# An expert layer in units of 32 rows: GpSimd makes the table of own rows, and TensorE turns the activation before the next rows

## What is computed

```
def hier_moe(h, w_rg, w_re, w_gate, w_up, w_down):
    ...
    act = jax.nn.silu(jnp.einsum('nd,edf->nef', xf, w_gate)) * jnp.einsum('nd,edf->nef', xf, w_up)
    act = act * comb.astype(act.dtype)[..., None]
    return jnp.einsum('nef,efd->nd', act, w_down).reshape(b, t, dm)
```

## Time and profile before

| what | value |
| --- | --- |
| median of three runs | 1614.38 us |
| the profiled execution | 1609.06 us, span 1607.3 us |
| TensorE matmul busy, whole span | 1386.7 us (86%) |
| VectorE busy | 682.8 us (42%) |
| GpSimd busy | 247.9 us (15%) |
| mean granted TensorE clock | 0.931 |
| weights and other loads of SyncE's hardware queue | 329.63 MB, 53.9% of 16 engines |
| loop over units | from about 1045 to 1584 us |
| gate/up matmuls (L2509) | 3328, 220.2 us |
| adds to x (L2597) | 156, 1215 ns each |

### The profile page before, as it was taken

How to read it: one execution, slowest core, us unless ns; L and a number is a source line. 1 busy time by engine, 2 the same in 40 slices (tenths; PEclk the granted TensorE clock), 3 DMA queues, 4 the chain that set the end, 5 groups by cost and what they waited for, 6 DMA issues and landing times. The chain is left out here.

```text
span 1607.3 us, 27516 instructions
## 1 busy us (share of the span) xinstructions
PE 1386.7 (86%) x10524; PEld 857.5 (53%) x10524; DVE 682.8 (42%) x1199; ACT 330.3 (21%) x734; POOL 247.9 (15%) x176
## 2 busy tenths in 40 slices
PE   7999999998999798778999899587889878887554
PEld 4478887777888566544544664433334333333221
DVE  3154333433553455574100223525455545654225
ACT  3001001222433244474000222111011111111102
POOL 0000000003000000000000000055344534453230
PEclk9999999999998699798999999789899989998877
DMA  9244547434430477104932234788958899859995
GB/s 346 104 171 168 188 146 259 149 120 171 172 112 7 144 233 233 47 1 172 310 111 105 96 114 187 298 321 367 377 245 326 353 421 375 367 191 418 421 422 217
DMA packets 108676, 360.96 MB, mean 225 GB/s; under 512 B 16462, under 2 KB 44150, under 8 KB 80290
## 3 DMA queue, kind: packets, MB, share of 16 engines
q1 hardware_dynamic: 104866, 329.63, 53.9%
q0 software_dynamic: 3232, 22.16, 3.8%
q10 hardware_dynamic: 512, 8.26, 1.4%
HBM read 482.68 MB, written 17.05 MB: 311 GB/s over the span
## 5 line engine op out<-in xcount | busy, mean ns | idle before, releaser
L2509 PE MATMUL bank<-ring,hT_e 128*32 128x256 f32 x3328 | 220.2, 415 | 87.6 <-DMA ring<-in_w_exp_up 50.1
L2597 DVE TENSOR_TENSOR x<-x,bank 128x1024 f32<-128x1024 f32 x156 | 183.1, 1215 | 262.8 <-PE bank L2496 256.7
L2465 POOL COPY ring<-ring 128x2048 f32 x104 | 194.9, 1902 | 246.8 <-DMA ring<-in_w_exp_gate 236.8
L2509 PEld LDWEIGHTS bank<-ring,hT_e 128*32 128x32 f32 x3328 | 113.2, 117 | 217.9 <-issue 168.9
L1853 PE MATMUL bank<-W,mixT 128*128 128x512 f32 x256 | 112.7, 600 | 1.6 <-DVE mixT L2088 1.6
L2525 PE MATMUL bank<-W,const 128*32 128x512 f32 x832 | 95.8, 596 | 13.1 <-ACT const L2555 11.2
L2496 PE MATMUL bank<-const,own_rows 32*128 32x512 f32 (+1 forms) x600 | 92.2, 685 | 6.7 <-DVE x L2597 6.7
L1853 PEld LDWEIGHTS bank<-W,mixT 128*128 128x128 f32 x256 | 48.9, 193 | 63.0 <-issue 60.8
L2551 ACT ACTIVATE gate<-bank 64x256 f32<-64x256 f32 x26 | 9.8, 376 | 321.9 <-PE bank L2509 321.9
L1833 POOL MEMSET mix<- 128x1024 f32 x1 | 1.0, 952 | 453.9 <-PE bank L1845 453.9
L517 PE MATMUL bank<-raw,hT 128*128 128x256 f32 (+1 forms) x288 | 65.2, 384 | 0.0
(11 more groups left out here) (424 smaller groups left out, 2069.7 us busy)
## 6 DMA issues: line engine op xcount, KB each, us to landing
ring<-in_w_exp_gate SPq DMA_DIRECT2D x108, 1024.0 KB
ring<-in_w_exp_up SPq DMA_DIRECT2D x104, 1024.0 KB
W<-in_w_exp_down SPq DMA_DIRECT2D x104, 1024.0 KB
raw<-in_w_in SPq DMA_DIRECT2D x10, 2048.0 KB
raw<-in_w_in SPq DMA_DIRECT2D x8, 2096.0 KB
W<-in_w_out SPq DMA_DIRECT2D x3, 4096.0 KB, 13.5
k_in<-in_cache_sel_k SPq DMA_DIRECT2D x64, 128.0 KB, 2.3
v_in<-in_cache_sel_v SPq DMA_DIRECT2D x64, 128.0 KB, 3.4
```

What stands on the lines that cost most here:

```text
L2465: pool.tensor_copy(w_g[:, quarter(q), :], held[:, quarter(q), :]).then_inc(g_copied[q], 1)
L2509: mm = pe.matmul(GATE[lane, 0:256], hT[:, k, q, :], (w_g if n < 2 else w_u)[:, c, cols], start=(c == 0), stop=(c == KC - 1))
L2597: ins = dve.tensor_tensor(x[rows, r, cols], x[rows, r, cols], src[rows, :], ALU.add)
```

## The change

VectorE's `find_rows` goes to GpSimd, where it first copies the unit's column of `token_of` to a tile of its own, waits for that copy, and compares. It stands behind the gather in GpSimd's loop, with a wait for the moves of the unit before; the semaphore `moved` begins at 3, so that this wait is the same for the first unit. On TensorE the activation is turned first and the next unit's rows after it. The last unit but one and the last are written out behind the loop.

```diff
+            row_token = side("row_token", [P, 1])
...
+                    def find_rows(turn):
+                        pool.tensor_copy(row_token[:, :], token_of[:, bass.ds(turn, 1)]).then_inc(token_picked, 1)
+                        pool.wait_ge(token_picked, turn + 1)
+                        pool.sem_inc(pool_passed, 1)
+                        pool.tensor_scalar(own_rows[:, :], token_no[:, :, :].rearrange("p k j -> p (k j)"), row_token[:, 0:1], None,
+                                           ALU.is_equal).then_inc(own_ready, 1)
+
...
                     gather(1)
+                    pool.wait_ge(token_ready, 1)
+                    pool.sem_inc(moved, 3)
                     with pool.Fori(0, before_last) as turn:
                         e = expert_of(turn + 1)
                         copy_gate(turn + 1, (0, 1), e)
                         pool.wait_ge(h_turned, turn + 2)
                         gather(turn + 2)
+                        pool.wait_ge(moved, turn * 3 + 3)
+                        find_rows(turn)
                         copy_gate(turn + 1, (2, 3), e)
-                    copy_gate(before_last + 1, range(4), expert_of(before_last + 1))
+                    copy_gate(before_last + 1, (0, 1), expert_of(before_last + 1))
+                    pool.wait_ge(moved, before_last * 3 + 3)
+                    find_rows(before_last)
+                    copy_gate(before_last + 1, (2, 3), expert_of(before_last + 1))
+                    pool.wait_ge(moved, before_last * 3 + 6)
+                    find_rows(before_last + 1)
...
-                    def down(turn):
+                    def down(turn, following=None):
                         pe.wait_ge(act_ready, turn + 1)
                         pe.sem_inc(pe_passed, 1)
                         for c in range(2):
                             mm = pe.transpose(ACT_T[:, c * 2 * UNIT:(c + 1) * 2 * UNIT], gate[UP, c:256:2], ident[UP, UP])
                         mm.then_inc(a_turned, 1)
+                        if following is not None:
+                            turn_rows(following)
                         pe.wait_ge(a_copied, turn + 1)
...
                     with pe.Fori(0, last) as turn:
-                        turn_rows(turn + 1)
-                        down(turn)
+                        down(turn, turn + 1)
                         gate_up(turn + 1, turn)
...
-                    def find_rows(turn):
-                        dve.tensor_scalar(own_rows[:, :], token_no[:, :, :].rearrange("p k j -> p (k j)"), token_of[:, bass.ds(turn, 1)], None,
-                                          ALU.is_equal).then_inc(own_ready, 1)
...
-                        dve.wait_ge(moved, turn * 3 + r + 1)
+                        dve.wait_ge(moved, turn * 3 + r + 4)
...
                     dve.sem_inc(added, 3)
+                    dve.sem_inc(token_ready, 1)
```

More of the change, by code:

```diff
@@ L2389, in trunk @@
             gathered = sem("e_gathered")
-            own_ready, moved, added, own_moved, summed = (sem("e_" + n) for n in ("own_ready", "moved", "added", "own_moved", "summed"))
+            own_ready, token_ready, token_picked, moved, added, own_moved, summed = (sem("e_" + n) for n in ("own_ready", "token_ready", "token_picked", "moved", "added", "own_moved", "summed"))
             junk = w_d[:, 0, :]
@@ L2607, in _ @@
                     dve.sem_inc(added, 3)
+                    dve.sem_inc(token_ready, 1)
                     drain(0)
                     activate(0)
-                    find_rows(0)
                     drain(1)
@@ L2617, in _ @@
                         add(turn - 1, 2)
-                        find_rows(turn)
                         drain(turn + 1)
@@ L2623, in _ @@
                     add(last - 1, 2)
-                    find_rows(last)
                     def add_last(k):
```

## The result

The changed kernel takes 1635.33 us (median of 4 runs, 1629.41 to 1640.10) against 1614.49 us (4 runs) before: a ratio of 1.0128, 95% interval 1.0086 to 1.0171. It is slower by 21 us. I had forecast slower by 11, inside a range, 1609 to 1637, that holds the measured time near its upper end.

What follows compares the result with a forecast made beforehand. The prediction took the restarts of the DMA weight stream, stretched by TensorE's late buffer releases, to bound the loop. Terms +14.0 + 4.4 − 5.3 − 2.4 = +10.7 us gave a median of about 1625 us, range 1609 to 1637.

Steps and rivals of the forecast that it cites:

- Rival C: Loop: TensorE's time counts at the hand-overs, so the removed waits return in full, 44.5 us, giving 1570; chance 0.06.
- Step 1: VectorE: with the compare gone, the drain follows the third add: −5.26 us after third units, −2.38 us at late hand-overs.
- Step 2: TensorE: transposing the activation first covers ScalarE's copy, −0.43 us per unit; rows reach PSUM 0.45 us later, without harm.
- Step 3: GpSimd: column copy, wait and compare cost 0.19 + 0.4 + 0.7 = 1.3 us, bounds 0.64 and 3.4.
- Step 4: GpSimd's queue: compare behind two gate copies and the gather; first move 7.7 us after the first landed gate quarter's copy.
- Step 5: TensorE after its pause: slower clock adds 1.0 us per unit; with the earlier lateness, six ordinary legs grow 14.0 us.
- Step 6: Two experts with a third unit: time from first gate copy to next expert's up-weight issue becomes 28.4 us, +4.4 us.
- Step 7: Elsewhere in the loop: later gate copies, added credit, changed thresholds and GpSimd work in units without landing waits cost nothing.
- rival D: GpSimd's compare takes longer, at an unfavourable rate or held by VectorE's adds: 12 us higher, 1637; chance 0.10.
- A: TensorE loses no clock after the pause: +3.5 us, 1618; chance 0.22.
- B: DMA stream: late buffer releases are free, so 14.0 us drops out, 1609 to 1611; chance 0.17.
- E: The effects cancel, or the compare's table is not what the first move waits for last: 1614; chance 0.05.

Runs made afterwards that it cites:

- Experiment 1: Kernel before with only the transposes reordered, activation first, then the next unit's rows; compare stays on VectorE ahead of the drain: 1606.42 us, ratio 0.9950.
- experiment 8: Changed kernel with GpSimd's compare at the start of its turn, ahead of the gate copies that wait for landings: 1605.41 us, ratio 0.9940.
- Experiment 9: Kernel before with GpSimd's gather held back by a 0.42 us fill, nothing of the change: 1609.66 us, ratio 0.9971.
- experiments 2: Changed kernel with GpSimd's compare ahead of its gather instead of behind it: 1615.49 us, ratio 1.0005.
- 7: Changed kernel with the table made once ahead of the loop, no compare or column copy in it, output not the reference's: 1606.29 us, ratio 0.9945.
- 6: Changed kernel with the three moves woven in after gate/up chunks 7, 12 and 15 instead of 3, 10 and 15: 1623.33 us, ratio 1.0047.
- Experiment 3: Changed kernel with GpSimd's order gate quarters 0 and 1, compare, gate quarters 2 and 3, gather: 1625.85 us, ratio 1.0064.
- experiment 10: Kernel of Experiment 1 with a 0.39 us fill ahead of VectorE's compare: 1607.04 us, ratio 0.9948.

## Why the prediction was right, and what was mis-sized

*What bounds the loop* held: the DMA stream restarts at T, and late releases stretch the leg. Removing 25.4 + 11.2 us of TensorE's waits gave some 8 us at most by the medians in any kernel here. Rival C, the full 44.5 us, was never in sight.

*Step 1*, the recovery of 5.3 and 2.4 us: measured −5.3 and −2.4. But I put it down to the compare leaving VectorE. Experiment 1 shows that the order of the transposes alone brings all of it, and experiment 8 that nothing is added by having both. *Step 2* is the one that was wrong in kind. I noted that the gather is released 0.45 us later and called it harmless; that delay is what lets the compare through. Experiment 9 has the delay alone, and with it the 5.3 and 2.4 us in legs and hand-overs. As both halves are in the change, the sum didn't suffer; a forecast of either half would have.

*Step 3*, F: 1.54 us instead of 1.3. The wait was 0.28 us, not 0.4, but the compare 1.09, not 0.7. It took longer per column than either of the earlier trace rows: (1.09 − 0.19) / 320 = 2.8 ns, against 0.8 and 2.1. The Trainium skill's "GPSIMD Engine Reference" (Elementwise — side-by-side cycle accounting) gives about 2.6 cycles per element for a two-input operation. This fits the two-input row (2.1 ns), but my estimate of 0.69 us from it for the compare, an operation with one input and a scalar, is low; the measurement decides.

*Step 4*, the place in the queue, is the cause, as forecast: experiments 2 and 8 move the compare and keep it, 7 takes it away, 6 takes the work from behind the wait, and each takes back the expected part. Experiment 3 moves it too and takes back 9.5 us only, since there the gather comes late. The first move came 8.22 us after G, against 7.7.

*Step 5*, the clock: 0.42 + 1.22 = 1.64 us after the pause in the unit shown. In the six units that set the ordinary legs the first move and the 56 matmuls behind it lose 1.54 to 2.78 us, 1.9 on average, with the two largest, 2.44 and 2.78, where D was over 12; I had 1.0. This rests on the rows; no kernel kept the clock up during the pause.

Steps 3 to 5 together are the term that was mis-sized. D came 11.72 us after T, not 10.3: 0.5 us of it from the later first move, 0.9 from the clock. That is 4.2 us later than before, not 2.7, and the six legs cost 20.0 us, not 14.0. My sign "D 9 to 11 us after T" was missed in all six (11.33 to 12.55). The price held on the average only: 20.0 / 6 / 4.19 = 0.79 us per us, against the 0.87 from the two long legs. Leg by leg it does not: with D 11.33 the leg of 27.23 us grew by 1.6 us, with D 11.41 another grew by 4.0 (1094.28 to 1123.84, before 1089.89 to 1115.42, D 7.63 in both before). What sets the leg beside D was not looked into. *Step 6*: +7.6 us instead of +4.4, from the same lateness. With 20.0 + 7.6 − 5.3 − 2.4 the forecast would have been +19.9. *Step 7* held: in the changed kernel TensorE never waited for a gate copy.

That the range holds 1635 is partly luck. The forecast's own range ended at 1633, and the 1637 came from rival D, a compare of over 2 us, which did not happen.

*Rivals*: A fell, the clock was lost. B fell, no leg of the six kept 25.6. E fell, the table ended the first move's wait in all eight. D fell: the 26 compares take 1.08 to 1.10 us. Only one of them ran beside one of VectorE's adds, but in experiment 8 it was 24 of 26, and all took 1.08 or 1.09, so those adds do not hold them.

## What to carry to other kernels

Before moving an instruction to an idle engine, write down its new queue with times from the trace: what it waits behind (landings above all), what now waits behind it, and the due time of its result. An engine that is 15% busy can still deliver late. And where a long and a short form of one instruction alternate, look for the neighbour in time before restructuring: here 0.4 us of delay in the right place (experiment 9) gained 4 us, and the move to the idle engine lost 21.

## What the runs showed of the hardware

- The ten compares of 4.51 us start 0.58 us *before* GpSimd's gate copies begin, and still end with them. At 0.37 us a free compare would be over before the copies begin, so they are not what held it first. A start 0.07 us after the gather's issue is free, and one at 0.44 or 0.67 us is held, through the copies that come after the gather (but see experiment 10).
- Without a gather in front, a compare that runs into a gate copy is not held, and the copy takes longer. In the kernel before three compares overlap the start of such a copy by 0.20, 0.23 and 0.28 us. Each takes 0.37 us, and the copies 1.96, 1.99 and 2.03 instead of 1.89. The last of the three:

```profile
1466.02 0.37 DVE L2590 TENSOR_SCALAR own_rows<-token_no,token_of 128x320 f32<-128x320 f32 x1
1466.11 2.03 POOL L2465 COPY ring<-ring 128x2048 f32 x1 [0.53 <-DMA ring<-in_w_exp_gate]
```

  The Trainium skill, "SBUF — State Buffer" (Who interferes with whom), has VectorE's `tensor_scalar`, when in a two-port mode, and GpSimd exclude each other for whole instructions, the first to issue winning. These three pairs fit that, and so does the end of a long compare. That a compare waits for two copies which begin after it goes beyond it, and no run here shows why.
- GpSimd's compare of 128 x 320 floats with one scalar per partition takes 1.09 us, VectorE's 0.37.
- After the pause of 4.30 us, with one quarter of gate/up ahead of it, TensorE ran the next 64 matmuls 1.64 us slower than at full clock. The granted clock in the two windows behind the pause (the windows table; the granted clock stands behind the five engines, in parts of 2.4 GHz: 0.72 and 1.00):

```profile
1199.00:1205.00 6.00, 5.85 (x64) 2.37 (x64) 2.35 (x2) 0.00 (x0) 6.00 (x4) 0.72 0.00 1
1205.00:1211.00 6.00, 5.73 (x70) 2.78 (x70) 3.98 (x4) 0.64 (x2) 1.25 (x1) 1.00 0.00 0
```

In the first the mean of 0.72 lies between the two levels, 1.2 and 2.4 GHz; in the second the full one is back. So this wait on TensorE cost over a third more than its own length.
